# Layer 2's gate projection turned around: weight tiles stationary, 256 token rows moving

## What is computed

```
def conformer_mixer(hn, w_in, b_in, w_dw, b_dw, ln_g, ln_b, w_out, b_out):
    proj = hn @ w_in
    ab = proj[..., :2 * CONV_WIDTH] + b_in
    z = proj[..., 2 * CONV_WIDTH:]
    a, g = jnp.split(ab, 2, axis=-1)
    u = a * jax.nn.sigmoid(g)
    u = depthwise causal convolution of u over 31 rows + b_dw
    u = jax.nn.silu(layer_norm(u, ln_g, ln_b))
    return (u * jax.nn.silu(z)) @ w_out + b_out
```

## Time and profile before

| | us |
|---|---|
| three timed runs: median (lowest to highest) | 840.38 (840.01 to 841.74) |
| span of the profiled execution | 838.3 |
| median less span (what lies around it) | 2.1 |
| TensorE busy with matmuls, share of the span | 828.1, 99% |
| VectorE, ScalarE, GpSimd busy | 713.9, 423.9, 341.8 |

### The profile page before, as it was taken

The page is one execution under the profiler, slowest core; times in us unless marked ns, Lnnn a source line. Parts: engine busy times, 40 slices in busy tenths (PEclk is TensorE's granted clock), DMA queues, the critical chain, the costliest instruction groups (busy, mean ns, idle before and its releaser), DMA issues.

```text
span 838.3 us, 10938 instructions
## 1 busy us (share of the span) xinstructions
PE 828.1 (99%) x3807; PEld 686.0 (82%) x3807; DVE 713.9 (85%) x1234; ACT 423.9 (51%) x584; POOL 341.8 (41%) x171
## 2 busy tenths in 40 slices
PE   9999999999999999999999999999999999999996
PEld 6888888888888888888888788888888888888884
DVE  5588799988999799979857649999999999898655
ACT  6744534464444645454446574544454554574541
POOL 0342005500440004400000298888888878893000
PEclk9999999999999999999999999999999999999998
DMA  9956556656567555747555485555555545567522
GB/s 318 317 177 203 172 159 192 194 163 196 155 194 210 185 157 162 233 155 251 180 187 191 146 299 195 180 182 199 199 169 187 198 154 199 200 226 245 189 94 100
DMA packets 97657, 161.62 MB, mean 193 GB/s; under 512 B 3316, under 2 KB 38484, under 8 KB 97108
## 3 DMA queue, kind: packets, MB, share of 16 engines
q1 hardware_dynamic: 97572, 161.13, 59.0%
q10 hardware_dynamic: 48, 0.02, 0.0%
HBM read 159.04 MB, written 2.10 MB: 192 GB/s over the span
## 4 chain that ended last, share of the span: by engine, by line
PE 97%; issue 1%; DMA 0%; ACT 0%; DVE 0%; SPq 0%; DVEq 0%; POOLq 0%; POOL 0%; ACTq 0%
PE acc L447 29%; PE acc L448 29%; PE acc L449 29%; PE X L457 1%; PE acc L432 1%; PE acc L434 1%; PE acc L433 1%; PE X L448 1%; PE X L447 1%; PE X L449 1%; PE acc L513 1%; PE acc L528 1%; DMA raw<-in_w_in 0%; PE X L573 0%; PE X L584 0%
## 5 line engine op out<-in xcount | busy, mean ns | idle before, releaser
L791 ACT ACTIVATE w_hi<-raw 128x1024 fp32r<-128x1024 f32 x282 | 298.5, 1060 | 339.2 <-PE acc L449 326.5
L447 PE MATMUL acc<-w_hi,xT_hi 128*128 128x512 f32 x864 | 338.8, 392 | 0.0
L449 PE MATMUL acc<-w_hi,xT_lo 128*128 128x512 f32 x864 | 336.6, 390 | 0.0
L448 PE MATMUL acc<-w_lo,xT_hi 128*128 128x512 f32 x864 | 336.4, 389 | 0.0
L1075 DVE TENSOR_TENSOR w_lo<-raw,w_hi 128x1024 fp32r<-128x1024 f32 x180 | 242.2, 1362 | 69.4 <-ACT w_hi L791 67.0
L1563 POOL TENSOR_TENSOR w_lo<-raw,w_hi 128x1024 fp32r<-128x1024 f32 x102 | 248.5, 2444 | 45.1 <-ACT w_hi L791 44.6
L449 PEld LDWEIGHTS acc<-w_hi,xT_lo 128*128 128x128 f32 x864 | 162.2, 188 | 33.9
L447 PEld LDWEIGHTS acc<-w_hi,xT_hi 128*128 128x128 f32 x864 | 162.3, 188 | 33.3 <-DVE xT_lo L1094 0.2
L448 PEld LDWEIGHTS acc<-w_lo,xT_hi 128*128 128x128 f32 x864 | 162.3, 188 | 32.8
L1365 DVE SCALAR_TENSOR_TENSOR X<-u_pad,taps,X 128x256 f32<-128x256 f32 x464 | 183.6, 477 | 3.5 <-ACT X L1004 3.5
L1526 POOL TENSOR_TENSOR small<-small 128x1 f32<-128x1 f32 (+1 forms) x7 | 4.3, 617 | 220.8 <-DVE small L1292 122.9
(11 more groups left out here) (159 smaller groups left out, 793.2 us busy)
## 6 DMA issues: line engine op xcount, KB each, us to landing
raw<-in_w_in SPq DMA_DIRECT2D x78, 1024.0 KB, 5.3
raw<-in_w_in SPq DMA_DIRECT2D x66, 512.0 KB, 4.4
raw<-in_w_out SPq DMA_DIRECT2D x32, 1024.0 KB, 5.1
gpost<-in_post_g SPq DMA_DIRECT2D x2, 1024.0 KB, 5.8
brow<-in_b_in SPq DMA_DIRECT2D x1, 2048.0 KB, 10.2
xrow<-in_x SPq DMA_DIRECT2D x4, 256.0 KB, 5.2
raw<-in_w_in SPq DMA_DIRECT2D x4, 256.0 KB, 4.6
xrow<-in_x SPq DMA_DIRECT2D x2, 512.0 KB, 9.3
```

The lines of the kernel that those rows point to most:

```text
L447: nc.tensor.matmul(a, hi[:, k, rows], w_hi[:, slot, i], start=(k == 0), stop=False)
L448: nc.tensor.matmul(a, hi[:, k, rows], w_lo[:, slot, i], start=False, stop=False)
L449: last = nc.tensor.matmul(a, lo[:, k, rows], w_hi[:, slot, i], start=False, stop=(k == KT - 1))
L791: nc.scalar.activation(w_hi[:, slot], raw[:, u % LOADS, 2 * half:2 * half + 2], ACT.Copy).then_inc(hi_ready[slot], 1)
```

## The change

Only z of layer 2 is made in another way. (1) `column_products` takes the place of `slice_products` in S_Z: a 128 by 128 tile of the weight slice is stationary and the 256 rows of xT move past it. A slice is now 2 channel tiles, 4 column groups and 3 products: 24 matmuls of 256 moving columns instead of 12 of 512. The result has channels on partitions already. (2) z's transposes go: `turn_gate` on VectorE and `last_gate_T` on TensorE. (3) The root lies along the free axis now, so it is spread: `scale_wide` on TensorE (two small float32 matmuls with the identity, after slice 12 of S_AG, the projections of a and g), a copy to rms_wide on ScalarE, and a multiplication of each block on VectorE (`scale_gate`). (4) ScalarE copies blocks out of PSUM without silu (`gate_columns`), and does silu in four further instructions of 128 by 1024 (`gate_silu`) after slices 28, 29, 29 of S_Z and slice 9 of S_OUT1. (5) FINAL_AT's last goes from 10 to 11, `final_low(2)` goes ahead of `gate(3)`, and zT moves to other SBUF addresses.

```
-FINAL_AT = (0, 4, 8, 10)
+FINAL_AT = (0, 4, 8, 11)
+GATE_SILU_AT = (28, 29, 29)
+LAST_GATE_AT = 9
+WIDE_AT = 12
...
+            def column_products(first, s):
+                slot = s % RING
+                par = ((first + s) // SLICES) % 2
+                pe.wait_ge(lo_ready[slot], rounds(first, 0, 0, s))
+                for i in range(SL_K):
+                    k = SL_K * (s % SLICES) + i
+                    for c in range(G):
+                        a = acc[:, par, c // 2, (c % 2) * SEQ:(c % 2 + 1) * SEQ]
+                        cs = slice(c * P, (c + 1) * P)
+                        nc.tensor.matmul(a, w_hi[:, slot, i, cs], xT_hi[:, k], start=(k == 0 and c % 2 == 0), stop=False,
+                                         skip_group_check=True)
+                        nc.tensor.matmul(a, w_hi[:, slot, i, cs], xT_lo[:, k], start=False, stop=False,
+                                         skip_group_check=True)
+                        last = nc.tensor.matmul(a, w_lo[:, slot, i, cs], xT_hi[:, k], start=False, stop=(k == KT - 1),
+                                                skip_group_check=True)
+                last.then_inc(w_used[slot], 1)
+            def scale_wide():
+                pe.wait_ge(rms_ready, 4)
+                for m in range(MT):
+                    last = nc.tensor.matmul(X[3][:, m * P:(m + 1) * P], rms[2][:, m:m + 1].to_broadcast([P, P]), ident[:],
+                                            start=True, stop=True)
+                last.then_inc(wide_done, 1)
...
-                slice_products(S_Z, 0, 0, s, xT_hi, xT_lo)
+                column_products(S_Z, s)
...
-                if s == 1:
-                    last_gate_T()
...
+                if s == WIDE_AT + 3:
+                    act.wait_ge(wide_done, 1)
+                    nc.scalar.activation(rms_wide[:], X[3][:, 0:SEQ], ACT.Copy).then_inc(wide_ready, 1)
...
+            def gate_columns(n):
+                s = SLICES * n + SLICES - 1
+                act.wait_ge(w_used[RING - 1], rounds(S_Z, 0, 0, s))
+                par = ((S_Z + s) // SLICES) % 2
+                for m in range(MT):
+                    last = nc.scalar.activation(zT[:, 4 * n + 2 * m:4 * n + 2 * m + 2],
+                                                acc[:, par, m].rearrange("p (t r) -> p t r", t=2), ACT.Copy)
+                last.then_inc(rows_out, 1)
+            def gate_silu(n):
+                act.wait_ge(z_scaled, n + 1)
+                z = zT[:, 4 * n:4 * n + 4]
+                nc.scalar.activation(z, z, ACT.Silu).then_inc(z_ready, 1)
...
+            def scale_gate(n):
+                dve.wait_ge(rows_out, 28 + n + 1)
+                if n == 0:
+                    dve.wait_ge(wide_ready, 1)
+                z = zT[:, 4 * n:4 * n + 4]
+                nc.vector.tensor_tensor(z, z, rms_wide[:].rearrange("p (o r) -> p o r", o=1).to_broadcast([P, 4, SEQ]),
+                                        ALU.mult).then_inc(z_scaled, 1)
...
-            turn_gate(0, (2, 3))
-            turn_gate(1, (0,))
+            scale_gate(1)
+            scale_gate(2)
             normalise(0)
             normalise(1)
-            turn_gate(1, (1,))
             gate(0)
             normalise(2)
             final_low(0)
-            turn_gate(1, (2, 3))
             gate(1)
             normalise(3)
             final_low(1)
-            turn_gate(2, range(4))
+            scale_gate(3)
             gate(2)
+            final_low(2)
             gate(3)
-            final_low(2)
             final_low(3)
```

More of the change, by code:

```diff
@@ L124, in build @@
         brow = at("brow", B + 16 * KB, [P, 2 * D])
-        z_row1 = at("z_row1", B + 16 * KB, [P, MT, D])
         y1 = at("y1", B, [P, MT, D])
-        zT = at("zT", B, [P, KT - G, SEQ])
+        zT = at("zT", B + 16 * KB, [P, KT, SEQ])
         gpost1 = at("gpost1", A + 16 * KB, [P, D])
@@ L152, in build @@
         uT = at("uT", C + 27 * KB, [P, G, SEQ])
+        rms_wide = at("rms_wide", C + 27 * KB, [P, SEQ])
         junk1 = at("junk1", C + 16 * KB, [P, NCOL])
@@ L249, in build @@
         norm_ready = sem("norm_ready")
-        zT_done = sem("zT_done")
-        z_turned = sem("z_turned")
+        wide_done = sem("wide_done")
+        wide_ready = sem("wide_ready")
+        z_scaled = sem("z_scaled")
+        z_ready = sem("z_ready")
         silu_ready = sem("silu_ready")
@@ L695, in two_blocks @@
                         conv_input_pair(2 * i, 0, first)
+                    if s == WIDE_AT and first:
+                        scale_wide()
             two_blocks(0, True)
@@ L722, in statistics_wide @@
                 last.then_inc(stat_ready, 1)
[L724 to L729, removed]
             for s in range(4 * SLICES):
@@ L1034, in _ @@
                 if s % SLICES == 3 and s > SLICES:
-                    n = s // SLICES - 1
-                    block_rows(S_Z, 0, 0, 8 * n + 7, z_row1[:, :, n * NCOL:(n + 1) * NCOL], rms[2], ACT.Silu)
+                    gate_columns(s // SLICES - 1)
                 for j in range(NG - 1):
@@ L1042, in _ @@
                                                  ).then_inc(c_ready, 1)
+                for n, at in enumerate(GATE_SILU_AT):
+                    if s == at:
+                        gate_silu(n)
                 if s in (30, 31):
@@ L1053, in _ @@
                 if s == 3:
-                    block_rows(S_Z, 0, 0, 31, z_row1[:, :, 3 * NCOL:4 * NCOL], rms[2], ACT.Silu)
+                    gate_columns(NG - 1)
+                if s == LAST_GATE_AT:
+                    gate_silu(NG - 1)
                 if s in FINAL_AT:
@@ L1402, in _ @@
             dve.wait_ge(bn_ready, MT * (NG - 1))
-            turn_gate(0, (0, 1))
+            scale_gate(0)
             row_stats(NG - 1)
@@ L1422, in gate @@
                 dve.wait_ge(silu_ready, n + 1)
[L1423 to L1431, removed]
+                dve.wait_ge(z_ready, n + 1)
+                c = cT[:, 4 * n:4 * n + 4]
+                last = nc.vector.tensor_tensor(c, c, zT[:, 4 * n:4 * n + 4], ALU.mult)
                 last.then_inc(t_ready, 1)
```

## The result

The changed kernel takes 844.68 us (median of four runs, 844.38 to 845.32) against 840.26 us before: ratio 1.0044, 95% interval 1.0032 to 1.0055, so 4.4 us slower. The profiled span went from 838.3 to 842.8 us, +4.5. That is inside the range on record (837.2 to 846.5) but not at the forecast 840.6: it is the figure of rival B, 845.0.

What follows compares the result with a forecast made beforehand. TensorE, 99% busy, was taken to bound the kernel. Matmuls +0.73, last_gate_T -0.88, scale_wide +0.45 and S_OUT1's start -0.11 gave +0.2 us: 838.5 us span, 840.6 us median, range 837.2 to 846.5 us.

Steps and rivals of the forecast that it cites:

- rival B: z-stage matmuls: a fixed price for each makes 256 columns cost 120 ns, +4.6 us in all, 845.0 us; chance 0.20.
- the load can be hidden down to 112 ns at least: z-stage stationary tiles: 24 layer 1 score passes took 111.8 ns each, load and matmul together, despite recorded loads of 188 ns.
- The term: z-stage matmuls: 768 of 256 columns at 114.3 ns replace 384 of 512 at 226.7 ns, +0.73 us.
- A: The forecast itself: 256-column z matmuls cost 112 to 116 ns, 838.8 to 841.9 us; chance 0.61.
- The surcharge: Matmuls on TensorE: an extra that grows with width, about 2.5 ns for each 128 columns.
- C: z-stage matmuls: no surcharge, 110 ns for 256 columns as the transposes step, 837.3 us; chance 0.09.
- D: z stage: tile loads become the bound, up to 188 ns a matmul, +56.8 us, 897 us; chance 0.04.
- `last_gate_T`: TensorE: eight transposes of z are removed, 0.88 us less.
- `scale_wide`: TensorE after slice 12 of S_AG: two added float32 matmuls, four passes at 112 ns, +0.45 us, no wait.
- the start of S_OUT1: First matmul of S_OUT1: TensorE's wait for VectorE's final_low(0) goes, -0.11 us.
- VectorE's saving: VectorE: transposes go, four multiplications come; busy time falls by 12 to 17 us, and the time should not follow.
- Rival E: Tail of the gate, S_OUT1 slice 10: low part late despite 0.9 us cover, 1.5 to 2.7 us, 842.1 to 843.3; chance 0.06.

## Why the prediction was right in its range and wrong in its term

The steps together:

| moving columns | stationary tile | step, ns |
|---|---|---|
| 512 | 128, fp32r | 226.7 |
| 512 | 64, fp32r | 229.7 |
| 384 | 128, fp32r | 173.3 |
| 256 | 128, fp32r (either side stationary) | 120.0 |
| 256 | 96, fp32r | 116.0 |
| 256 | 64 or 32, fp32r | 113.4, 113.3 |
| 256 | 128, bf16 | 113.3 |
| 128 | 128, fp32r | 111.7 |
| 512, granted clock 0.5 | 128, fp32r | 426.7 |
| 384, granted clock 0.5 | 128, fp32r | 320.0 |

**The step that failed** is "the load can be hidden down to 112 ns at least", as I used it: I took the 111.8 ns of the scores as the price of load and matmul together, and added 2.5 for a wider matmul. But 128 fp32r columns take the same 111.7, so nothing says that the 111.8 held the price of 256 columns; and the 2.5 was read from recorded durations, which are modelled. What the runs showed in its place: a full fp32r load and a 256-column matmul, each good for 112 to 113 ns apart, take 120.0 side by side. The term was forecast at 114.3 ns (+0.73 us) and measured 120.0 (+5.11 us by the steps, +4.84 in the stage); that is the whole miss. The range was right only because it had been drawn wide enough to hold rival B: the time lies outside A's own 838.8 to 841.9.

**What held.** The surcharge does grow with the width: 113.3 at 256 columns with a light load, half of 226.7, where I had 114.3 and C had 110. The load is no bound at its recorded length (D): loads follow each other every 111.7 ns in a stage of 768 as in a run of 24. `last_gate_T`, `scale_wide` and the start of S_OUT1 came out within some hundredths. VectorE's saving of 12.4 us was worth nothing but the 0.11. (12 to 17 had been forecast, though 1.1 to 3.6 us for a `scale_gate` give 7 to 17; the four took 2.42, 1.22, 1.22 and 3.42 us.) Rival E did not happen: `low` of slice 10 ended near 772.63 + 3.49 / 3 = 773.8, and TensorE began that slice at 747.40 + 27.2 = 774.6; a cover of 0.8 us, for which 0.9 less the signals had been worked out.

```profile
772.63 3.49 DVE L1121 TENSOR_TENSOR w_lo<-raw,w_hi 128x1024 fp32r<-128x1024 f32 x3
...
774.63 0.39 PE L452 MATMUL acc<-w_hi,vT_hi 128*128 128x512 f32 x1
```

**Rival B** had the number and half of the mechanism. N / 2.4 + 13.3 fits full tiles at 256, 384 and 512 columns to 0.1 ns, but it isn't a fixed price: at 256 columns half of it goes with a narrower tile or with bf16, and at the lower clock all of it (320.0 and 426.7 ns). By the rule of the Trainium skill that I had weighed (TensorE: Matmul & The Clock Gate, Back-to-back issue gap), which the section gives for a matmul by itself, without a load, the stage would have grown by 1.0 us; no run here has 256 columns at its 109.2 ns.

**What stays open.** Whether it is the load, as I think, that lifts 113.3 to 120.0, and why the two would hinder each other when both are about 112 ns long, why 3.3 ns are left at 384 columns (173.3 against three quarters of 226.7, 170.0), and why narrower tiles make the 512-column step longer. The runs show when the price is paid, not in which part of the engine.

## What to carry to other kernels

Turning a product around changes the width of the moving operand, and where TensorE is the chain that is the first thing to price: the same multiplications in 256-column matmuls took 6% longer here than in 512-column ones: 5.1 us, against 0.88 us of transposes saved. Read the price of a narrow matmul from one that has the same width and the same kind of load; two prices measured apart, for the load and for the matmul, don't say what they cost together when they are about equal. And work taken from an engine that isn't on the chain is worth only the wait that the chain had for it: 0.11 us here.

## What the runs showed of the hardware that I had not expected

256-column fp32r matmuls with full fp32r tiles step at 120.0 ns, although full loads can follow each other every 111.7 and the matmul takes 113.3 with a tile of 64 columns or less. The order of sums, the side that is stationary, and loading the same tile again make no difference to it. Alternating fp32r and bf16 matmuls of 256 columns took 360.0 ns for three, although bf16 alone takes 113.3 each. fp32r matmuls of 128 columns, each with a full load, step at 111.7 ns: half the columns save only 8.3 ns. At a granted clock of 0.5 fp32r matmuls took N / 1.2 ns and nothing more: 320.0 for 384 columns, 426.7 for 512.
